# A hybrid decoder layer on one core: the single item's rows gathered in the last pair's first gates, the first gather begun by tiles, and small moves at the start, at a bias split and at the end

## What is computed

```python
h = rms_norm(x, norm_mix)
proj = h @ w_in                      # 24 column pieces of 256 are used here
#   a gated delta rule (4 heads) and an mLSTM (4 heads), in chunks,
#   each behind a causal convolution and a SiLU, then
y = sigmoid(gate_gdn) * (o_a @ w_up_gdn) + sigmoid(gate_ml) * (o_b @ w_up_ml)
x = x + y @ w_out
hf = rms_norm(x, norm_ffn)
top_val, top_idx = top_k(hf @ w_router + b_router, 4)      # of 32 experts
gates = softmax(top_val)
gu = xb @ w_gate_up[e] + b_gate_up[e]                      # xb: the rows that chose e
gate, up = minimum(gu[..., ::2], 7), clip(gu[..., 1::2], -7, 7)
y_e = (gate * sigmoid(1.702 * gate) * (up + 1)) @ w_down[e] + b_down[e]
out = rms_norm(x + sum of gates * y_e, norm_final)
```

## Time and profile before

| | us |
|---|---|
| three runs | 1223.25, 1225.66, 1227.62 |
| median | 1225.66 |
| the profiled execution, its own time | 1222.7 |
| its span, first to last instruction | 1220.9 |

### The profile page before, as it was taken

One profiled execution on the slowest core, in us unless ns is written; L12 is line 12 of the kernel. 1 busy time (PEld: TensorE's weight loads), 2 busy tenths in 40 slices (PEclk: granted clock), 3 DMA queues, 4 the chain that ended last, 5 costly groups with the idle time before them and its releaser, 6 DMA issues.

```text
span 1220.9 us, 13386 instructions
## 1 busy us (share of the span) xinstructions
PE 1150.0 (94%) x5643; PEld 591.0 (48%) x5643; DVE 308.6 (25%) x732; ACT 126.5 (10%) x215; POOL 18.0 (1%) x43
## 2 busy tenths in 40 slices
PE   9999799999999999999989898999999988899896
PEld 8788688865434343443434243434434333434342
DVE  2579712434422021211202020202112020202021
ACT  3641011001000000000000000000000000000001
POOL 1010200000000000000000000000000000000000
PEclk9999899999999999999999999999999999999999
DMA  9854553476999999999999999999999999999994
GB/s 256 250 169 140 199 173 129 162 319 223 399 424 428 428 428 428 426 427 429 428 427 426 429 428 428 427 427 428 427 428 426 428 428 427 428 428 427 428 422 188
DMA packets 63629, 444.66 MB, mean 364 GB/s; under 512 B 8669, under 2 KB 33489, under 8 KB 37969
## 3 DMA queue, kind: packets, MB, share of 16 engines
q1 hardware_dynamic: 57968, 438.38, 87.3%
q0 software_dynamic: 1184, 3.43, 1.0%
q10 hardware_dynamic: 4416, 1.99, 0.7%
HBM read 442.31 MB, written 1.46 MB: 363 GB/s over the span
## 4 chain that ended last, share of the span: by engine, by line
PE 58%; DMA 32%; DVE 6%; SPq 2%; issue 1%; ACT 1%; POOL 0%; ACTq 0%; DVEq 0%
DMA ring<-in_w_down 30%; PE bank L882 21%; PE bank L940 13%; PE bank L569 9%; PE bank L862 3%; PE bank L805 2%; PE bank L979 2%; SPq L443 2%; PE bank L775 1%; PE bank L764 1%; DVE hn L1315 1%; PE bank L874 1%; DVE ring L1312 1%; DVE cvm L1198 1%; PE bank L954 1%
## 5 line engine op out<-in xcount | busy, mean ns | idle before, releaser
L882 PE MATMUL bank<-ring,cvg 128*64 128x512 f32 x2112 | 462.2, 593 | 11.1 <-DMA ring<-in_w_gate_up 10.8
L882 PEld LDWEIGHTS bank<-ring,cvg 128*64 128x64 f32 x2112 | 151.9, 137 | 301.3 <-issue 273.1
L940 PE MATMUL bank<-ring,cvg 128*64 128x512 f32 x1024 | 233.2, 611 | 31.7 <-DMA ring<-in_w_down 31.7
L1577 DVE TENSOR_SCALAR cvm<-bank 128x512 f32<-128x512 f32 x33 | 22.8, 692 | 649.0 <-PE bank L882 649.0
L569 PE MATMUL bank<-ring 128*128 128x256 f32 x768 | 171.1, 383 | 0.3 <-DVE cvm L1198 0.3
L940 PEld LDWEIGHTS bank<-ring,cvg 128*64 128x64 f32 x1024 | 79.3, 141 | 183.4 <-issue 183.4
L569 PEld LDWEIGHTS bank<-ring 128*128 128x128 f32 x768 | 145.7, 192 | 20.4 <-issue 0.8
L1961 ACT ACTIVATE cvm<-cvm 128x512 f32<-128x512 f32 x33 | 20.8, 631 | 499.3 <-DVE cvm L1577 499.3
L862 PEld LDWEIGHTS bank<-ltm,hn 128*128 128x128 f32 x544 | 66.6, 196 | 7.3 <-issue 7.1
L862 PE MATMUL bank<-ltm,hn 128*128 128x128 f32 x544 | 66.9, 281 | 0.0
L979 PE MATMUL bank<-vb,ltm 128*128 128x512 f32 x128 | 57.7, 593 | 0.0
(11 more groups left out here) (334 smaller groups left out, 526.4 us busy)
## 6 DMA issues: line engine op xcount, KB each, us to landing
ring<-in_w_gate_up SPq DMA_DIRECT2D x128, 2048.0 KB, 32.7
ring<-in_w_down SPq DMA_DIRECT2D x58, 2048.0 KB, 35.6
ring<-in_w_in SPq DMA_DIRECT2D x24, 1024.0 KB, 6.7
ring<-in_w_down SPq DMA_DIRECT2D x12, 1024.0 KB, 34.0
ring<-in_w_out SPq DMA_DIRECT2D x4, 1024.0 KB, 4.9
ring<-in_w_up_ml SPq DMA_DIRECT2D x2, 1024.0 KB, 5.0
ring<-in_w_up_gdn SPq DMA_DIRECT2D x2, 1024.0 KB, 5.5
xs<-in_x SPq DMA_DIRECT2D x2, 512.0 KB, 4.6
```

The source lines that it names most:

```text
L882: mm = pe.matmul(B[4 + half][side * SLOTS:(side + 1) * SLOTS, :], xT[:, k, e * SLOTS:(e + 1) * SLOTS], w[:, (k % 2) * PIECE + at:(k % 2) * ...
L940: mm = pe.matmul(B[6 + half][e * SLOTS:(e + 1) * SLOTS, :], actT[:, e, at:at + SLOTS], by_block(double(of[e]), 4)[:, j, half * HALF:(half ...
L1577: dve.tensor_scalar(g2, both[:, :, :, 0], SWIGLU_LIMIT, None, ALU.min).then_inc(sem("glu_g_ready"), 1)
```

## The change

1. **Start.** `mean_square`, `root` and `normalised` of the first tile run before those of the second, the copy of the turned parameters comes later on DVE, and TensorE's second filler (8 matmuls) goes.
2. **Bias split.** The multiplication that signals `kd_ready` moves ahead of the whole bias split.
3. **Start of the experts.** `open_gate_up(0, 0)` moves ahead of the last turn and router step. The first gather goes tile by tile: the first tile's half is put where the filler of 6 matmuls stood, before the counting of the second tile; two matmuls with zero weights open the banks for it. DVE takes the gathered rows before it forms the gate weights instead of after.
4. **Single item.** Its gather (now 64 columns wide) moves from the end of the last pair into that pair's first gates, after the second double; its one-hot table and its `xT` get places of their own.
5. **End.** A square root of a spare tile is added on ACT after the last sigmoid.

```diff
-            keep_busy(8)
             for t in range(T):
                 pe.wait_ge(sem("hn_ready"), t + 1)
...
-            turn_x2(1, 1)
-            router(1, 1)
...
+            def gather_lone():
+
+                pe.wait_ge(sem("onehot_ready"), (N_GROUPS - 1) * 2 * T + 4 * T)
+                pe.wait_ge(sem("turned_copied"), (N_GROUPS - 1) * 2)
+                pe.wait_ge(sem("scat_ready"), N_GROUPS - 1)
+                for k in range(KC):
+                    for t in range(T):
+                        by_row = hn[:, t, :].rearrange("s (i p j) -> s i j p", p=P, j=2)
+                        mm = pe.matmul(B[6 + k // 4][:, (k % 4) * P:(k % 4) * P + SLOTS], by_row[:, k // 2, k % 2, :],
+                                       onehot_lone[:, t, :], start=(t == 0), stop=(t == T - 1))
+                    if k % 4 == 3:
+                        mm.then_inc(sem("gathered"), 1)
...
+                    if n == N_GROUPS - 1 and e == 0 and i == 1:
+                        gather_lone()
...
-                    pe.wait_ge(sem("xT_ready"), n * 2 + 4)
+                    pe.wait_ge(sem("xT_ready"), n * 2 + (6 if n == N_GROUPS - 2 else 4))
...
+            def open_gather(b):
+                pe.matmul(B[6 + b], zero[:, :].to_broadcast([3 * E, P]), bgu[:, 0:HALF], start=True, stop=False,
+                          skip_group_check=True)
+
+            def gather_tile(t, b):
+
+                pe.wait_ge(sem("onehot_ready"), 2 * t + 2)
+                pe.wait_ge(sem("h2_ready"), t + 1)
+                by_row = hn[:, t, :].rearrange("s (i p j) -> s i j p", p=P, j=2)
+                for k in range(KC // 2 * b, KC // 2 * (b + 1)):
+                    mm = pe.matmul(B[6 + b][:, (k % 4) * P:(k % 4 + 1) * P], by_row[:, k // 2, k % 2, :],
+                                   onehot[:, t, :], start=False, stop=(t == T - 1), skip_group_check=True)
+                if t == T - 1:
+                    mm.then_inc(sem("gathered"), 1)
+
             pe.wait_ge(sem("bgu_split"), 1)
             open_gate_up(0, 0)
-            keep_busy(6, 2)
+            turn_x2(1, 1)
+            open_gather(0)
+            router(1, 1)
+            gather_tile(0, 0)
+            open_gather(1)
+            gather_tile(0, 1)
             pe.wait_ge(sem("chosen_ready"), T)
             pe.matmul(ranks[1], ones[:, :], chosen[:, 0, :], start=True, stop=False)
             pe.matmul(ranks[1], striu[:, :], chosen[:, 1, :], start=False, stop=True).then_inc(sem("ranks_done"), 1)
             keep_busy(3, 2)
-            pe.wait_ge(sem("onehot_ready"), 2 * T)
-            pe.wait_ge(sem("h2_ready"), T)
-            gather(0, 0)
-            gather(0, 1)
+            gather_tile(1, 0)
+            gather_tile(1, 1)
...
+            mean_square(0, 0)
+            normalised(0, 0, "hn_ready")
+            mean_square(0, 1)
             dve.wait_ge(sem("prm_turned"), 1)
             link(dve.tensor_copy(prmT[:, :], B[4][:, 0:96]))
-            for t in range(T):
-                mean_square(0, t)
-            for t in range(T):
-                normalised(0, t, "hn_ready")
+            normalised(0, 1, "hn_ready")
...
-            dve.wait_ge(sem("expert_bias"), 48)
-            split_bias(0)
-            bias_left(0)
             dve.wait_ge(sem("k_turned"), 1)
             dve.wait_ge(sem("ex8_ready"), 1)
             dve.tensor_tensor(kd0[:, :, :], B[4].rearrange("p (h i) -> p h i", h=H),
                               bc(ex8[:, 0:H].unsqueeze(2), [P, H, P]), ALU.mult).then_inc(sem("kd_ready"), 1)
+            dve.wait_ge(sem("expert_bias"), 48)
+            split_bias(0)
+            bias_left(0)
...
+            take_xT(0, 0, 1)
+            take_xT(0, 1, 2)
...
-            take_xT(0, 0, 1)
-            take_xT(0, 1, 2)
...
             sigmoid(N_GROUPS, 0)
+            se.activation(rstd[:, :], rstd[:, :], ACT.Sqrt).then_inc(sem("root_warm"), 1)
             se.wait_ge(sem("act_turned"), N_GROUPS * 2 + 1)
```

More of the change, by code:

```diff
@@ L245, in decoder_layer @@
         picked = sb("picked", [3 * E, 2, SLOTS], BF16)
+        zero = sb("zero", [3 * E, 1], BF16)
         load8 = sb("load8", [P, E])
@@ L285, in decoder_layer @@
         scat_left = onehot
+        onehot_lone = ltm[:, 3, :, 0:SLOTS]
+        xT_lone = cvm[:, 2 * HC - 2:2 * HC, :].rearrange("p a (b s) -> p (a b) s", s=SLOTS)
         actT_left = act[:, 1, :]
@@ L875, in open_gate_up, with gate_up_row @@
                                   start=True, stop=False, skip_group_check=True)
-            def gate_up_row(k, e, w, after=None):
+            def gate_up_row(k, rows, w):
                 for half in range(2):
@@ L881, in gate_up_row @@
                         at = side * FE + half * HALF
-                        mm = pe.matmul(B[4 + half][side * SLOTS:(side + 1) * SLOTS, :], xT[:, k, e * SLOTS:(e + 1) * SLOTS],
+                        mm = pe.matmul(B[4 + half][side * SLOTS:(side + 1) * SLOTS, :], rows,
                                        w[:, (k % 2) * PIECE + at:(k % 2) * PIECE + at + HALF], start=False,
@@ L915, in gate_up @@
                     for k in (2 * i, 2 * i + 1):
-                        mm = gate_up_row(k, e, double(d))
+                        mm = gate_up_row(k, xT_lone[:, k, :] if n == N_GROUPS else xT[:, k, e * SLOTS:(e + 1) * SLOTS], double(d))
                     if not keeps:
@@ L1047, in _ @@
                 scatter(n - 1)
-                pe.wait_ge(sem("onehot_ready"), n * (2 * T) + 4 * T)
-                gather(n + 1, 1)
-                pe.wait_ge(sem("turned_copied"), n * 2 + 1)
-                gather(n + 1, 0)
+                if n < N_GROUPS - 1:
+                    pe.wait_ge(sem("onehot_ready"), n * (2 * T) + 4 * T)
+                    gather(n + 1, 1)
+                    pe.wait_ge(sem("turned_copied"), n * 2 + 1)
+                    gather(n + 1, 0)
                 pe.wait_ge(sem("xT_ready"), n * 2 + 3)
@@ L1142, in _ @@
             link(dve.memset(mv_s[:, :, :, DH:DH + 1].rearrange("p t h c -> p (t h) c"), 1.0))
+            link(dve.memset(zero[:, :], 0.0))
             link(dve.memset(select[:, :], 0.0))
@@ L1748, in _ @@
                 dve.wait_ge(sem("gathered"), n * 2 + 2)
-                make_onehot(n + 1)
-                make_weighted(n)
+                if n < N_GROUPS - 1:
+                    make_onehot(n + 1)
+                else:
+                    for t in range(T):
+                        dve.tensor_scalar(onehot_lone[:, t, :], siota[:, :], posx[:, t, LONE:LONE + 1], None,
+                                          ALU.is_equal).then_inc(sem("onehot_ready"), 2)
+                make_weighted(n)
+                if n == N_GROUPS - 1:
+                    for b in range(2):
+                        dve.wait_ge(sem("gathered"), n * 2 + 3 + b)
+                        dve.tensor_tensor(xT_lone[:, 4 * b:4 * b + 4, :],
+                                          B[6 + b].rearrange("p (k s) -> p k s", k=4)[:, :, 0:SLOTS],
+                                          bc(ffn_rows[:, 4 * b:4 * b + 4].unsqueeze(2), [P, 4, SLOTS]),
+                                          ALU.mult).then_inc(sem("xT_ready"), 1)
                 glu(n, 0)
@@ L1753, in _ @@
                 make_picked(n + 1)
-                take_xT(n + 1, 1, n * 2 + 3)
-                take_xT(n + 1, 0, n * 2 + 4)
+                if n < N_GROUPS - 1:
+                    take_xT(n + 1, 1, n * 2 + 3)
+                    take_xT(n + 1, 0, n * 2 + 4)
                 take_scat(n, 6)
```

2 lines of the change are left out of this document (1 added, 1 removed).

## The result

| | before | after |
|---|---|---|
| runs, us | 1223.25, 1224.90, 1225.66, 1227.62 | 1208.77, 1209.04, 1210.95, 1212.26 |
| median, us | 1225.28 | 1209.99 |
| profiled span, us | 1220.9 | 1207.2 |

The ratio of after to before is 0.9877, with a 95% interval of 0.9852 to 0.9901: faster by 15.1 us (12.1 to 18.1). The profiled executions differ by 13.7 us. The forecast was 1213.4, a gain of 12.3.

The account below looks back on a forecast made before the run. The transfer stream after the first release was taken as the bound, with TensorE's path before it counting in full. Terms -9.6 - 1.3 - 1.4 = -12.3 gave a median of 1213.4 us, range 1208.5 to 1218.5.

Parts of the forecast that it names:

- The bound: From first release at 302.6 us, 182 doubles take 892 us; TensorE time before it counts, later time is covered.
- Bias split, -9.6: At L726 after proj(13): TensorE's 7.6 us stall for DVE's kd goes, and full clock there saves 2.0 us.
- What is late next: After the bias split: the next common wait, base_loaded, and DVE's work behind it would not delay TensorE.
- The room of 7.8 us: At base_loaded: DVE sees it at 143.84 us, TensorE asks for it at 151.6 after proj(16).
- Start, -1.3: First norms and transposes: L614 starts at 11.0 us instead of 12.29; bounds -1.4 and 0.
- Start of the experts, TensorE -1.7, stream -1.4: Half the gather ahead of the counting: first gates 1.7 us earlier, transfers gain 1.4; bounds -0.3 and -1.7.
- the discount of 0.3 for the stream: At the experts' start: transfers gain 1.4 of TensorE's 1.7 us, since some of 16 engines work through release waits.
- Single item and end, 0: Last pair and end: TensorE's 3.92 us turn into waiting and the added root gains nothing; 0 us.
- The table's step: ACT's end: the 1.28 us table load stays ahead of the old root despite the added one; 0, bound -0.6.
- The 1.2 GHz through the whole projection: Slower rival: without filler TensorE stays throttled from 8 us, pieces taking 13.8 instead of 6.9 us; 1237 us, 3%.
- the next wait: Rival: base_loaded or DVE late behind the bias split takes part of the 9.6 us; half gives 1218.2 us, 7%.
- The first rival: One or two more clock falls of 1.7 us at the start or last pairs; 1215.2 to 1216.7 us, 10%.

Follow-up runs that it names:

- the filler: Changed kernel with 16 more filler matmuls on TensorE just ahead of the first release: 1214.91 us, ratio 0.9941 to the kernel before.
- the repeated gather: Changed kernel with half of one gather repeated five times in the eighth pair, after the first release: 1210.53 us, ratio 0.9905 to the kernel before.
- the filled stall: Kernel before, with 28 filler matmuls on TensorE in its stall between proj(13) and L726: 1221.89 us, ratio 0.9991.
- the start alone: Kernel before with only the part at the start, including removal of the 8 filler matmuls: 1222.71 us, ratio 0.9988.
- double later: Changed kernel with the second double fetched ahead issued two weight pieces later on SyncE's queue: 1209.40 us, ratio 0.9900 to the kernel before.
- two queues: Changed kernel with four of the eight small base_out_copy transfers issued by ACT instead of POOL: 1210.53 us, ratio 0.9892 to the kernel before.
- no loop: Changed kernel without ACT's conditional loop over further experts: 1211.64 us, ratio 0.9907 to the kernel before.
- start filled: Changed kernel with the second double two pieces later and filler in TensorE's two idle stretches ahead of 10 us: 1210.90 us, ratio 0.9900 to before.

## Why the prediction came out right

**The bound.** The stream from the first release to the end was the bound, as argued. The prediction's 892 us for it stand in the fourteen profiles as 891.9 to 894.4, wherever the release lies, and the filler and the repeated gather separate the two kinds of TensorE time by 4.35 against 0.2 us. The release moved by 13.25 us and the last landing by 14.2; the 0.9 between them lies within that spread and is no gain of the change.

**Bias split, -9.6.** Issues show -9.76, and alone 11.3 (9.4 to 13.2). The stall of 7.6 and the clock's 2.0 (1.5 to 2.7 by the filled stall) were sized right, on one profile of before in which the low clock happened to be short.

**What is late next.** This is the one step that failed. The room of 7.8 us took POOL's transfers as fixed in time. Only their first issue was nearly so; they then ran in threes through landings beside a weight piece and a double that came 11.9 us earlier, and the last was 5.7 us later. 7.8 - 5.7 leaves 2.1, the 2.13 us that TensorE had gained before took these, and TensorE waited, 0.52 us by the issues. It was named as a rival, and came to a twentieth of the bias split's gain. That it was so little was luck: the forecast had counted 7.8 us as free, and all of it was used.

**Start, -1.3.** Measured -1.64 at L616, and 1.5 (0.4 to 2.6) alone. 0.3 of the 1.64 is no part of the change: the parameters landed that much earlier, so TensorE's turn began at 7.72 instead of 8.0. The fall of the clock was expected and came once, for 3.4 us; that it was not the longer one of the start alone was luck, worth 1.6 us. The prediction weighed a rule of the Trainium skill (TensorE: Matmul & The Clock Gate, Part 1), that the default state is throttled and activity releases it, and priced it at the whole gain of the start. The measurement decides against that price: the start alone was 1.5 us faster without its filler, and filling its idle stretches gave nothing back.

**Start of the experts, TensorE -1.7, stream -1.4.** TensorE had -1.88, the time alone 2.2 (1.1 to 3.3). Whether the discount of 0.3 for the stream was right is not shown: the spread of 2.5 us behind the release hides it.

**Single item and end, 0.** Alone 1.0001 (0.9989 to 1.0013). At the end TensorE waits five times for transfers (0.28 to 1.41 us), where it had waited once: the time won turned into waiting. The table's step was right too: the loop puts the second load back.

**The sum, -12.3.** The span moved by -13.7. Against the sum that is +0.5 for the wait, -0.2 for the bias split, -0.3 for the start, -0.5 between 72 and 81 us, -0.5 for the experts' start with the discount, -0.9 in the stream behind it and +0.5 behind the last landing; none is larger than one fall of the clock. The median's 15.1 is more than 13.7, but five kernels that differ from the changed one by things worth 0.5 us at most (double later, repeated gather, two queues, no loop, start filled) stand at 0.989 to 0.991, 11 to 13 us, and before ran at 1222.5 to 1223.6 in the longer series beside them. So the distance of 3.0 us between profile and median, which the prediction kept, was in part chance.

**The rivals.** No rival of the prediction took the place of the forecast. The 1.2 GHz through the whole projection did not come (0.65 at 14 us, 0.50 at 16 us, and from there each piece took its 6.9 us), and the next wait took 0.52 us and not half of 9.6. The first rival, a further fall of the clock, is not in this profile, but it is in others with the same start (6.8 us of low clock there in three of eight) and with the same start of the experts (one at 280 us, with the filler ahead of the release and with two queues). So in a single execution it is chance that decides between this rival and the forecast.

## To carry to other kernels

Find the moment from which a stream of transfers never rests; TensorE's microseconds ahead of it count in full, those behind it turn into waits. When a stall goes, list what used that quiet time: small transfers on another queue are not fixed in time, they slow down when the weights move in beside them. And a wait must be checked against all parts of a change together, for each part takes from the same room.

## What the runs showed of the chip

- POOL had three of these eight transfers under way at a time: the next was issued 0.34 to 0.35 us after the third landed, in each of the executions listed, whatever DVE did. ACT issued four within 1.4 us (131.12 to 132.50) and did not wait for a landing (the first at 134.47).
- Stretches at 1.2 GHz come at some places in one execution and not in another, of code that is the same up to there. At 280 to 285 us the granted clock was 0.67 or 0.66 in three kernels and 1.00 in the changed one, and the issues behind it came 1.3 to 1.6 us later. Ahead of the first release there were from one such place to three in a profile, and what falls in TensorE's work there counts; in the kernel with the repeated gather one at 340 to 345 us delayed the releases by 1.66 us, and the landings did not move with it (0.64 us later than after's ahead of it, 0.4 to 0.7 behind it). This is as large as most parts of this change, so one profile does not tell what a part of 1 to 2 us is worth; that takes the median of many executions or the same issue in many profiles.
- In this kernel the table of functions is loaded again behind ACT's conditional loop, whose body uses another function, even though the loop runs no time: with the loop the added root bought nothing, without it the load was gone.
